# First attention's reciprocals on GpSimd, and one weight load of the expert stage behind a gather

## What is computed

```python
s = jnp.einsum("bhmqd,bhmkd->bhmqk", qb, kb) * scale      # m: two maps per head
s = jnp.where(tk <= tq, s - slopes * dist, -jnp.inf)
p = jax.nn.softmax(s, axis=-1)
a = p[:, :, 0] - lam * p[:, :, 1]
outs.append(jnp.einsum("bhqk,bhkd->bhqd", a, vb))
...
o = rms_norm(o, attn_sub_norm_g[l]) * (1.0 - lam_init)
...
for e in range(N_EXPERTS):
    act = jax.nn.silu(t @ w_gate[e]) * (t @ w_up[e]) * gates[:, e:e + 1]
    y = y + act @ w_down[e]
```

## Time and profile before

| what | value |
|---|---|
| median of 3 runs | 2307.84 us (2303.1 to 2309.04) |
| profiled execution, its time | 2308.68 us |
| its span | 2306.9 us |
| PE busy | 2230.6 us, 97% of the span |
| DVE, ACT, POOL busy | 1358.4, 1074.1, 512.5 us |
| mean DMA | 102 GB/s, 236.41 MB |

### The profile page before, as it was taken

One profiled execution on the slowest core, in us unless ns is written; L12 is line 12 of the kernel. 1 busy time (PEld: TensorE's weight loads), 2 busy tenths in 40 slices (PEclk: granted clock), 3 DMA queues, 4 the chain that ended last, 5 costly groups with the idle time before them and its releaser, 6 DMA issues.

```text
span 2306.9 us, 30184 instructions
## 1 busy us (share of the span) xinstructions
PE 2230.6 (97%) x11284; PEld 1770.4 (77%) x11284; DVE 1358.4 (59%) x2094; ACT 1074.1 (47%) x1722; POOL 512.5 (22%) x514
## 2 busy tenths in 40 slices
PE   7999999989999999999999999999999999999998
PEld 6877567856666766888878888887788878888886
DVE  5884685346666744766337775445477327776354
ACT  4312784325555656554334443436655344445242
POOL 2167242112223334211220011102211220002001
PEclk9999999989999999999999999999999999999999
DMA  5210210359999964111110013122111110013112
GB/s 132 87 37 1 74 74 10 124 211 341 360 357 351 331 252 145 46 28 37 49 39 15 1 37 146 50 79 84 37 37 37 34 47 19 12 38 146 38 55 101
DMA packets 146491, 236.41 MB, mean 102 GB/s; under 512 B 44096, under 2 KB 100672, under 8 KB 134464
## 3 DMA queue, kind: packets, MB, share of 16 engines
q1 hardware_dynamic: 135136, 209.53, 25.7%
q0 software_dynamic: 8928, 16.80, 3.0%
q10 hardware_dynamic: 2304, 8.39, 0.9%
HBM read 208.98 MB, written 41.42 MB: 109 GB/s over the span
## 4 chain that ended last, share of the span: by engine, by line
PE 71%; DMA 9%; DVE 4%; ACT 3%; issue 3%; POOL 1%; SPq 1%; POOLq 0%; DVEq 0%; ACTq 0%
PE ps L106 13%; PE ps L108 13%; PE ps L107 13%; DMA h_dram<-X 9%; PE ps L96 7%; PE ps L2139 2%; PE ps L1884 1%; PE ps L1754 1%; PE ps L2092 1%; PE ps L2091 1%; PE ps L2093 1%; PE ps L2130 1%; PE ps L2129 1%; PE ps L2127 1%; PE ps L2126 1%
## 5 line engine op out<-in xcount | busy, mean ns | idle before, releaser
L108 PE MATMUL ps<-HT_hi,WF_lo 128*128 128x512 f32 x800 | 311.8, 390 | 0.0
L106 PE MATMUL ps<-HT_hi,WU_hi 128*128 128x512 f32 x704 | 282.5, 401 | 6.7 <-POOL WF_lo L1109 1.9
L107 PE MATMUL ps<-H_lo,WU_hi 128*128 128x512 f32 x704 | 274.1, 389 | 0.0
L107 PE MATMUL ps<-WT_lo,HT_hi 128*128 128x512 f32 x656 | 255.4, 389 | 0.0
L1109 POOL TENSOR_TENSOR WF_lo<-WF,WU_hi 128x1024 fp32r<-128x1024 f32 x42 | 112.6, 2680 | 434.8 <-ACT WU_hi L1392 434.8
L106 PE MATMUL ps<-W_hi,HT_hi 128*128 128x512 f32 x472 | 186.0, 394 | 2.3 <-ACT WF L1667 2.3
L108 PE MATMUL ps<-W_hi,MIX_lo 128*128 128x512 f32 x480 | 187.2, 390 | 0.0
L108 PEld LDWEIGHTS ps<-HT_hi,WF_lo 128*128 128x128 f32 x800 | 150.2, 188 | 31.9
L106 PEld LDWEIGHTS ps<-HT_hi,WU_hi 128*128 128x128 f32 x704 | 132.2, 188 | 40.1 <-issue 3.8
L107 PEld LDWEIGHTS ps<-H_lo,WU_hi 128*128 128x128 f32 x704 | 132.3, 188 | 29.0 <-issue 2.9
L107 PEld LDWEIGHTS ps<-WT_lo,HT_hi 128*128 128x128 f32 x656 | 123.3, 188 | 25.1 <-issue 0.5
(11 more groups left out here) (486 smaller groups left out, 5575.6 us busy)
## 6 DMA issues: line engine op xcount, KB each, us to landing
WT<-in_w_gate SPq DMA_DIRECT2D x31, 1024.0 KB, 7.8
WT<-in_w_up SPq DMA_DIRECT2D x31, 1024.0 KB, 10.9
MIX<-in_w_down SPq DMA_DIRECT2D x31, 1024.0 KB, 10.1
WF<-in_w_in SPq DMA_DIRECT2D x48, 512.0 KB, 3.7
WT<-in_w_out SPq DMA_DIRECT2D x6, 2048.0 KB, 8.0
H<-h_dram SPq DMA_DIRECT2D x24, 512.0 KB, 10.9
H<-in_x SPq DMA_DIRECT2D x16, 512.0 KB, 7.5
h_dram<-H SPq DMA_DIRECT2D x16, 512.0 KB, 3.3
```

Source lines behind the costliest of these rows:

```text
L106: pe.matmul(o, lh, rh, start=(i == 0), stop=False)
L107: pe.matmul(o, lh, rl, start=False, stop=False)
L108: mm = pe.matmul(o, ll, rh, start=False, stop=(i == last))
```

## The change

Two edits. In the first attention, VectorE's reciprocals and the product behind them go to GpSimd, as a power with exponent -1 and a product with two scalars; GpSimd takes them up as soon as a block's second exponential is written, and normalises block g - 3 behind them. A new counter, `scaled_sum`, stands for the two results: VectorE's combination and ScalarE's scaling wait for it. A constant tile `minus_one` is set once at the start. In the expert stage, SP issues both loads of tile 1's gate and up weights behind the wait for the first gather.

```diff
@@ sync
             load_gu(0, 0)
             load_d(0, 0)
-            load_gu(0, 1, (0,))
             sp.wait_ge(m_hg[0], 16)
-            load_gu(0, 1, (1,))
+            load_gu(0, 1)
             sp.wait_ge(pg_ready, 2 * NT)
             load_d(0, 1)
@@ gpsimd
+            pool.memset(minus_one, -1.0)
...
-            for q in range(NB):
-                o, ssq, rsq = on[:, q % 3, :], sm[:, q % 4, 8:9], sm[:, q % 4, 9:10]
-                pool.wait_ge(o_cp, q + 1)
-                chain.link(pool.tensor_scalar(ssq, ssq, 1.0 / P, EPS, ALU.mult, ALU.add))
-                chain.link(pool.tensor_tensor(rsq, ssq, mhalf[:, 0:1], ALU.pow))
-                pool.tensor_scalar(o, o, rsq, None, ALU.mult).then_inc(o_n, 1)
+            for g in range(NB + 3):
+                if g < NB:
+                    t = sm[:, g % 4, :]
+                    pool.wait_ge(e_ready, 2 * g + 2)
+                    settle(pool, settled)
+                    chain.link(pool.tensor_tensor(t[:, 6:8], t[:, 4:6], minus_one, ALU.pow))
+                    pool.tensor_scalar(t[:, 7:8], t[:, 7:8], t[:, 4:5], lam4[:, 4:5], ALU.mult, ALU.mult).then_inc(scaled_sum, 1)
+                if g >= 3:
+                    q = g - 3
+                    o, ssq, rsq = on[:, q % 3, :], sm[:, q % 4, 8:9], sm[:, q % 4, 9:10]
+                    pool.wait_ge(o_cp, q + 1)
+                    settle(pool, settled)
+                    chain.link(pool.tensor_scalar(ssq, ssq, 1.0 / P, EPS, ALU.mult, ALU.add))
+                    chain.link(pool.tensor_tensor(rsq, ssq, mhalf[:, 0:1], ALU.pow))
+                    pool.tensor_scalar(o, o, rsq, None, ALU.mult).then_inc(o_n, 1)
@@ scalar
                     act.wait_ge(o_ready, q + 1)
+                    act.wait_ge(scaled_sum, q + 1)
@@ vector
-                    dve.wait_ge(e_ready, 2 * q + 2)
-                    chain.link(dve.reciprocal(t[:, 6:8], t[:, 4:6]))
-                    chain.link(dve.scalar_tensor_tensor(out=t[:, 7:8], in0=t[:, 7:8], scalar=t[:, 4:5], in1=lam4[:, 4:5], op0=ALU.mult, op1=ALU.mult))
+                    dve.wait_ge(scaled_sum, q + 1)
                     dve.scalar_tensor_tensor(out=sS[0][q % 3][:, 0:W], in0=sS[1][q % 2][:, 0:W], scalar=t[:, 7:8], in1=sS[0][q % 3][:, 0:W],
                                              op0=ALU.mult, op1=ALU.add).then_inc(a_ready, 1)
```

More of the change, by code:

```diff
@@ L258, in program @@
         lam4 = stat[:, 32:40]
+        minus_one = stat[:, 40:42]
         sm = sb("sm", [P, 4, 16])
@@ L445, in program @@
         rw_in, rt_ready = sem("rw_in"), sem("rt_ready")
+        scaled_sum = sem("scaled_sum")
         rx, rm_ready, rp_ready, tab_in, tab_ready, experts_set = (
```

## The result

The kernel with the change takes 2314.44 us (median of 13 runs, 2310.55 to 2316.23), the one before 2307.15 us on the same chip (13 runs, 2303.1 to 2309.86). The ratio is 1.0028, 95% interval 1.0020 to 1.0036: 7.3 us slower by the medians, and just outside the range given, 2300.5 to 2314.

What follows compares the result with a forecast made beforehand. TensorE's matmuls were taken to hold most of the chain, the scatter-add into `h_dram` 9%. From 2308.7 us, attention +3.1 and experts -5.0 gave 2306.8, 2306 against the median; forecast 2306.5 us, range 2300.5 to 2314.

Steps and rivals of the forecast that it cites:

- attention +3.1: First attention: sum of late blocks +2.6, VectorE's saving -3.1 and GpSimd falling back +3.6 us.
- experts -5.0: Experts' start: earlier landing of the first gather, -3.4 us, plus a kept TensorE clock, -1.6 us.
- Price of power and product: First attention, GpSimd: two-column power put at 0.70 us, one-column product with scalars from memory at 0.30 us.
- estimate of 0.76 us for the pair by a factor of two: First attention: GpSimd about twice as slow as VectorE, so the pair 0.76 us and the attention about even.
- Late wide blocks, +2.6 us: First attention, four 1024-column blocks: combination starts 1.25 us behind the sum instead of 0.61, costing 2.6 us.
- VectorE's relief, -3.1 us: First attention: VectorE saves 0.45 us in each of seven blocks where it is on the chain, 3.1 us.
- GpSimd not free, +3.6 us, ends 0 to 7: First attention: GpSimd, 88% taken, falls back in short steps and TensorE's transposes wait; +3.6 us.
- Rival 1: First attention: a dearer power makes GpSimd the bound, every block waiting; +15 us, 2319; chance 0.1 with milder forms.
- Gather, -3.4 us: Experts' start: without the gate load ahead, the first gather lands at 512.0 instead of 515.39 us, saving 3.4.
- Clock, -1.6 us: Experts' first tile: shorter idle may keep TensorE's clock, worth 2.5 us, counted at two thirds, 1.6 us.
- Rival 4: Experts' second tile: gate weights come too late and TensorE waits what it saved at the first; 2311, chance 0.08.
- Rival 2: Experts' start: gate load does not hold up the gather, attention's loss stands almost alone; 2311 us, chance 0.15.

Runs made afterwards that it cites:

- e1: The change with only its attention edit, the expert stage's loads as before; 1.0034 of the kernel before, 2315.60 against 2308.28 us.
- e7: e1 with the normalisation's scale and shift left out on GpSimd; attention stretch 123.6 us, one execution, profile only.
- e12: Whole change without the normalisation's scale and shift, 1/128 kept as a square root in the 128x128 product; 2307.81 against 2308.84 us, ratio 0.9993.
- e13: Whole change with the normalisation's scale and shift moved between GpSimd's power and product; ratio to before 1.0006, attention stretch 127.2 us.
- e3: Kernel before with reciprocals and product left out on any engine, factors set to one; attention stretch 123.5 us, one execution, profile only.
- e2: Kernel before with only the gather edit, the second tile's gate load moved behind the first gather's wait; ratio 0.9993.
- e4: Kernel before with the second tile's gate and up loads, then the first tile's down weights, behind the first gather's wait; ratio 0.9998.
- e11: Whole change with only 12 of 32 pairs (128-, 384-, 640-column blocks) on GpSimd, the rest on VectorE; 2307.05 against 2308.08 us, ratio 0.9995.
- e10: Whole change with GpSimd's order turned round, the 128x128 product of block g-4 straight behind the pair of block g; ratio to before 1.0037.
- e9: e1 with GpSimd's order turned round, the 128x128 product of block g-4 straight behind the pair of block g; ratio to before 1.0041.
- e8: e1 with a second, unread 128x2 power on GpSimd behind each pair's product; attention stretch 135.5 us, one execution, profile only.

## Why the prediction was wrong

It had the mechanisms nearly all, and two sizes wrong, both in the same direction: attention +3.1 forecast and 8.4 in the stretch (7.6 at the same clock at the start, 7.3 to 7.8 in the time of e1), experts -5.0 forecast and -1.3 to -1.6, which is not clear of nothing.

- **Price of power and product**: right, 0.72 and 0.34 us for 0.70 and 0.30. The row of one column was the nearer one. The estimate of 0.76 us for the pair by a factor of two was too low: 1.06.
- **Late wide blocks, +2.6 us**: the delay is there (1.38 us for 1.25), but in e7 and e12 it costs nothing at the attention's end, and in e13 the stretch falls while it grows.
- **VectorE's relief, -3.1 us**: borne out up to the last combination (e3: 2.4 us, 3.1 against e2), but only 0.4 to 1.2 us at the last write, behind a stretch at half clock. The term took it for granted that what is gained at the last combination lasts to the end.
- **GpSimd not free, +3.6 us, ends 0 to 7**: this is the term that failed. Against e3, which has neither the late blocks nor GpSimd's pair, the change is 7.9 us later at the last combination and 8.8 at the last write, where this term and the one for late blocks gave 6.2 together; and of VectorE waiting for GpSimd I forecast 4 to 7 us and it was 19.9. I carried the stalls of 0.31 us a block over from the trace of before, as if they were a property of the stage. They are a property of the order. Now they are (641 - 192) + (708 - 612) + (627 - 569) = 0.60 us, since the end of the product starts VectorE's long operation and GpSimd's next one together. With the 2.8 us of work that is 3.4 us against a pace of 3.54, 96% and not 88%, and the bursts that I had costed at half their worst made a backlog that ran into the tail, where the clock then fell too. e13, with the stall moved to where it costs less, gives back 5.1 us. Rival 1 named this end (every block waits for GpSimd), with its condition on the power's price; the price stayed low and the state came about by the stall, in a milder form. It had a tenth.
- **Gather, -3.4 us**: 3.3 us between the two profiled executions, but 2.0 between the means of six kernels each. The 8.28 us I started from was one execution, and the longest of its kind.
- **Clock, -1.6 us**: kept through the first tile in after, e4, e11 and e12 (transposes 1.16 us, L96 1.88), lost in e2, e10 and e13 (1.54 to 1.89); about as often as I had put it, and not to be had at will. In the change itself it fell one tile later, which gave 1.7 us back (5.37 for 3.70).
- **Rival 4**, weights late at the second tile, had 0.08 and came in part: 2.23 us of waiting in place of 1.38 in the profile after, where I had written that they just fit. The up weights, issued at 521.28, were used at 533.31, 12.0 us later; I had allowed 9. With the clock that fell behind this wait it is 2.5 us. The other kernels with the edit wait 1.38 to 1.47 us there and lose time too: of the 3.0 us gained on the mean by the second tile's transposes, 1.7 are gone by the first scatter's issue. By which waits was not separated.
- **Rival 2** (the gather is not held up by the gate load) falls in its full form, since 2.0 us did go. How much the turns from packet to packet of which the Trainium skill (DMA: Bandwidth & Descriptors, Queues, rings and completion order) speaks have to do with the rest, no run here shows; with 2 MB less ahead of it, in e4, the gather still took 4.99 us to the transposes.

## What to carry to other kernels

When a value is moved to another engine, look at what its completion releases on both engines at once: if the consumer's instruction locks the producer out, the producer's next short instruction pays the consumer's whole length, in every block. Fill that place with something that waits for nothing and starts first, or take the small instruction into a gap that exists, but keep each result's due time. And before a saving is counted from a wait, see in more than one execution how long that wait is, and whether TensorE's clock stood the same in the stretches compared.

## What the runs showed of the hardware

- Two starts about 0.1 us apart decide a stall. A GpSimd instruction that starts 0.05 us behind a two-input combination of VectorE stands until its end: 20 of 32 in the profile after, 0.91 us on the mean for one of 0.19. Of 110 that started 0.02 to 0.12 us behind in all 15 profiles, three did not stand (in e9 one took its 0.19 us). One that starts 0.03 to 0.1 us ahead of it is not lengthened: 22 of 32 powers in e8 at 0.704 us, 17 of 32 in e13 at 0.566. Two 128x128 products that had started only 0.01 us ahead (e11, e13) stood as well, 1.55 and 1.02 us.
- In that order VectorE is held up little or not at all. In e8 the combination of 896 columns that started 0.08 us behind GpSimd's power took 1.15 us, as in the profile after, where it came first, and all 32 sum to 26.15 us against 26.13. Behind the 128x128 product it is longer, but not by the product's length: 0.09 us in e9, and 0.05 to 0.12 us in all 43 cases of the 15 profiles in which the product, 0.61 us long, started 0.03 to 0.11 us ahead; the earlier it had started, the less. By the Trainium skill (SBUF — State Buffer, SBUF: two separate sides) whichever starts first has the ports for its whole instruction, and the other fully blocks. By that rule VectorE would have stood for the rest of the power's 0.70 us or of the product's 0.61; the traces show the full block in one direction and not in this one.
- On GpSimd a power of 128x2 takes 0.72 us and one of 128x1 0.57, a 128x1 product with two scalars from memory 0.34 and with two constants 0.19. VectorE did the work of the pair in 0.16 and 0.22 us.
